# First layer's modulation in eight blocks of 256 shift and 256 scale columns, the first group of projections walking one block behind

## What is computed

```python
def mixer_layer(x, mod, norm_w, w_in, ...):
    shift, scale, gate = jnp.split(mod, 3, axis=-1)
    xn = rmsnorm(x, norm_w) * (1.0 + scale[:, None, :]) + shift[:, None, :]
    proj = xn @ w_in
    ...
# per layer, for both groups of tokens:
mod = jax.nn.silu(c) @ w_mod[l] + b_mod[l]        # w_mod[l]: 2048 x 6144 (shift, scale, gate)
```

## Time and profile before

| | us |
|---|---|
| median of three runs (2228.12 to 2229.08) | 2228.21 |
| profiled execution, whole | 2229.19 |
| its span | 2227.4 |
| PE busy in the span | 2174.2 |
| DVE busy | 1381.7 |
| ACT busy | 679.4 |

### The profile page before, as it was taken

How to read it: one execution, slowest core, us unless ns; L and a number is a source line. 1 busy time by engine, 2 the same in 40 slices (tenths; PEclk the granted TensorE clock), 3 DMA queues, 4 the chain that set the end, 5 groups by cost and what they waited for, 6 DMA issues and landing times.

```text
span 2227.4 us, 34005 instructions
## 1 busy us (share of the span) xinstructions
PE 2174.2 (98%) x13257; PEld 1922.4 (86%) x13257; DVE 1381.7 (62%) x2701; ACT 679.4 (31%) x1196; POOL 186.0 (8%) x125
## 2 busy tenths in 40 slices
PE   5999999999999999999989999999999999999998
PEld 2578877888999999999988888887799999999998
DVE  5469777986565666666457454555446666666654
ACT  4332222321343333533134222232133333344312
POOL 0000000000000000423321000000000000042331
PEclk9999999999999999999989999999999999999999
DMA  9988587664432333664444645444343333366444
GB/s 353 381 299 299 184 262 229 204 212 138 122 104 79 94 101 111 198 195 134 119 135 141 192 139 177 146 127 129 88 128 91 101 100 101 97 197 196 133 123 146
DMA packets 353200, 362.49 MB, mean 163 GB/s; under 512 B 17062, under 2 KB 259580, under 8 KB 352444
## 3 DMA queue, kind: packets, MB, share of 16 engines
q1 hardware_dynamic: 323536, 317.65, 45.8%
q10 hardware_dynamic: 29548, 43.25, 5.4%
HBM read 301.97 MB, written 58.88 MB: 162 GB/s over the span
## 4 chain that ended last, share of the span: by engine, by line
PE 91%; DVE 3%; ACT 2%; DMA 1%; issue 1%; ACTq 0%; SPq 0%; DVEq 0%
PE psP L732 32%; PE psP L767 20%; PE psP L784 10%; PE psT L742 8%; PE psO L973 5%; PE psP L904 3%; PE psO L946 2%; PE psT L915 2%; PE psO L693 1%; PE psT L973 1%; PE psT L650 1%; PE psO L650 1%; PE psO L797 1%; PE psP L985 1%; PE psP L674 1%
## 5 line engine op out<-in xcount | busy, mean ns | idle before, releaser
L732 PE MATMUL psP<-x_high,high 128*128 128x512 f32 x1024 | 413.1, 403 | 5.6 <-DVE x_low L1689 5.0
L732 PE MATMUL psP<-x_high,low 128*128 128x512 f32 x1024 | 400.7, 391 | 0.0
L732 PE MATMUL psP<-x_low,high 128*128 128x512 f32 x1024 | 400.7, 391 | 0.0
L1634 DVE SCALAR_TENSOR_TENSOR macc<-mraw,cond,macc 128x384 f32<-128x384 f32 (+1 forms) x960 | 389.7, 480 | 0.0
L1175 ACT ACTIVATE high<-raw 128x1024 fp32r<-128x1024 f32 x128 | 135.4, 1058 | 520.8 <-PE psT L742 507.0
L732 PEld LDWEIGHTS psP<-x_high,high 128*128 128x128 f32 x1024 | 193.2, 189 | 65.3 <-issue 24.0
L767 PE MATMUL psP<-x_high,high 128*128 128x320 f32 x1024 | 243.3, 319 | 0.5 <-issue 0.5
L767 PE MATMUL psP<-x_high,low 128*128 128x320 f32 x1024 | 233.3, 309 | 0.0
L767 PE MATMUL psP<-x_low,high 128*128 128x320 f32 x1024 | 232.7, 308 | 0.0
L732 PEld LDWEIGHTS psP<-x_high,low 128*128 128x128 f32 x1024 | 193.1, 189 | 41.6
L732 PEld LDWEIGHTS psP<-x_low,high 128*128 128x128 f32 x1024 | 193.5, 189 | 39.0 <-issue 1.9
(11 more groups left out here) (312 smaller groups left out, 3508.1 us busy)
## 6 DMA issues: line engine op xcount, KB each, us to landing
raw<-in_w_in_dram SPq DMA_DIRECT2D x128, 512.0 KB, 4.7
wmod<-in_w_mod_dram SPq DMA_DIRECT2D x32, 1024.0 KB, 9.5
mraw<-in_w_mod_dram SPq DMA_DIRECT2D x64, 512.0 KB, 4.3
mraw<-in_w_mod_dram SPq DMA_DIRECT2D x32, 1024.0 KB, 7.0
raw<-in_w_in_dram SPq DMA_DIRECT2D x32, 1024.0 KB, 6.1
raw<-in_w_out_dram SPq DMA_DIRECT2D x64, 512.0 KB, 4.4
old<-x_scratch SPq DMA_DIRECT2D x64, 320.0 KB, 3.0
proj_scratch<-stage ACTq DMA_DIRECT2D x64, 256.0 KB, 3.2
```

The source lines that it names most:

```text
L732: mm = pe.matmul(latent_ps[m], w[:, kk, cols], x[:, k, 0:DEC], start=(k == 0 and w is whole and x is x_high), stop=(k == KT - 1 and w is r ...
L1634: m = dve.scalar_tensor_tensor(acc[:, v, 0:width], mraw[hf][:, k, 0:width], c, acc[:, v, 0:width], ALU.mult, ALU.add)
```

## The change

The columns are cut in another way: block t now has the 256 shift columns and the 256 scale columns of the two input tiles 2t and 2t + 1. Each quarter of a block is loaded by two DMAs of 512 KB, one for each part, whose rows are 256 columns long. Two input tiles can be made ready after each block, where four were after every second. On PE, block 1 moves into the loop, with three pieces behind it; blocks 2 to 6 have five pieces each between and behind their quarters; block 7 has one behind each quarter, one more before its turn, and seven behind that. The turn of block t - 1 comes behind the first quarter of block t. ACT's and DVE's loops run over eight blocks of two tiles.

```diff
--- before.py
+++ after.py
@@ -72,20 +72,15 @@
 MOD_T = 3 * KT
 MOD_N = 512
 MOD_CHUNKS = 2 * D // MOD_N
-BLOCKS = KT // (MOD_N // P)
-BLOCK_K = MOD_N // P
-BLOCK_C = BLOCK_K // CHUNK_K
-
-
-def mod_at(t):
-
-    return (KT if t % 2 == 0 else 0) + t // 2 * BLOCK_K
+MOD_K = MOD_N // P
+BLOCKS = MOD_CHUNKS
+BLOCK_K = KT // BLOCKS
+assert BLOCK_K == CHUNK_K and MOD_K == 2 * BLOCK_K
 
 
 PIECES = GROUP_T + 1
 
-PIECES_AFTER, PIECES_LAST = [0, 1, 1, 1, 1, 1, 1, 0], 4
-assert sum(PIECES_AFTER) + PIECES_LAST == BLOCK_C * PIECES and len(PIECES_AFTER) == 8
+PIECES_AFTER = [[0, 0, 0, 3]] + [[1, 1, 1, 2]] * (MOD_CHUNKS - 3) + [[1, 1, 1, 1]]
 SAVES = 8
 SAVE_K = KT // SAVES
 SAVE_AT = {CHUNKS + RING + 2 * i: i for i in range(SAVES)}
@@ -335,7 +330,7 @@
             return pair[at // 2][:, at % 2 * KT // 2:(at % 2 + 1) * KT // 2, :].rearrange("p a b -> p (a b)")\
                 .rearrange("p (k n) -> p k n", n=GROUP_N)
         rs_ps = [psT[:, 0:512], psO[:, 512 + 2 * P:512 + 3 * P]]
-        mod_ps, mod_back = [psT[:, 512:512 + MOD_N], psO[:, 0:MOD_N]], psO[:, 512:512 + 2 * BLOCK_K]
+        mod_ps, mod_back = [psT[:, 512:512 + MOD_N], psO[:, 0:MOD_N]], psO[:, 512:512 + 2 * MOD_K]
         block = ctx.enter_context(nc.Block())
 
         q_back = psP[1][:, 0:TOK]
@@ -381,8 +376,10 @@
 
                 for q in range(4):
                     sp.wait_ge(s[f"wmod_used{q}"], t + SEED)
-                    sp.dma_start(wmod[q][:], wm[:, q * KT // 4:(q + 1) * KT // 4, mod_at(t) * P:mod_at(t) * P + MOD_N])\
-                        .then_inc(s[f"wmod_in{q}"], 16)
+                    for part in range(2):
+                        at = part * D + t * BLOCK_K * P
+                        sp.dma_start(wmod[q][:, :, part * BLOCK_K * P:(part + 1) * BLOCK_K * P],
+                                     wm[:, q * KT // 4:(q + 1) * KT // 4, at:at + BLOCK_K * P]).then_inc(s[f"wmod_in{q}"], 16)
 
             def front_chunk(l, n):
 
@@ -645,7 +642,7 @@
 
                 if q == 0 and t >= 2:
                     pe.wait_ge(s["mod_row"], t - 1)
-                pe.wait_ge(s[f"wmod_in{q}"], t * 16 + 16)
+                pe.wait_ge(s[f"wmod_in{q}"], t * 32 + 32)
                 for k in range(KT // 4):
                     mm = pe.matmul(mod_ps[t % 2][32 * k:32 * k + 2, :], cond[:, q * KT // 4 + k, :], wmod[q][:, k, :],
                                    start=(q == 0), stop=(q == 3), skip_group_check=True)
@@ -655,7 +652,7 @@
 
                 pe.wait_ge(s["mod_row"], t + 1)
                 pe.wait_ge(s["mod_taken"], t + SEED)
-                for j in range(BLOCK_K):
+                for j in range(MOD_K):
                     mm = pe.matmul(mod_back[:, 2 * j:2 * j + 2], mod_rows[t % 2][:, j * P:(j + 1) * P], fold[:, 0:2],
                                    start=True, stop=True)
                 mm.then_inc(s["mod_turned"], 1)
@@ -678,12 +675,6 @@
             pe.wait_ge(s["x_squared"], 2 * TT)
             pe.matmul(rs_ps[0], ones[:], r_a[:, 0:DEC], start=True, stop=True)
             pe.matmul(rs_ps[1], ones[:], r_a[:, DEC:TOK], start=True, stop=True).then_inc(s["stat_summed"], 1)
-            for q in range(4):
-                mod_quarter(1, q)
-                if q == 0:
-                    pe.wait_ge(s["x_squared"], 2 * TT + 2)
-                    mod_turn(0)
-            mod_turn(1)
 
             def gate_ranks():
 
@@ -837,19 +828,19 @@
 
                     pe.wait_ge(s["x_taken"], KT)
                     piece = 0
-                    for t in range(2, MOD_CHUNKS):
+                    for t in range(1, MOD_CHUNKS):
                         for q in range(4):
                             mod_quarter(t, q)
-                            if t % 2 == 1 and q == 0:
+                            if q == 0:
+                                if t == 1:
+                                    pe.wait_ge(s["x_squared"], 2 * TT + 2)
                                 mod_turn(t - 1)
-                            for _ in range(PIECES_AFTER[t % 2 * 4 + q]):
+                            for _ in range(PIECES_AFTER[t - 1][q]):
                                 block_piece(piece)
                                 piece += 1
-                        if t % 2 == 1:
-                            mod_turn(t)
-                            for _ in range(PIECES_LAST):
-                                block_piece(piece)
-                                piece += 1
+                    block_piece(piece)
+                    piece += 1
+                    mod_turn(MOD_CHUNKS - 1)
                     while piece < CHUNKS * PIECES:
                         block_piece(piece)
                         piece += 1
@@ -1137,8 +1128,9 @@
             def mod_take(t):
 
                 act.wait_ge(s["mod_turned"], t + 1)
-                act.activation(mod_raw[:, 0, mod_at(t):mod_at(t) + BLOCK_K, :].rearrange("p a b -> p (a b)"), mod_back,
-                               ACT.Copy).then_inc(s["mod_taken"], 1)
+                act.activation(mod_raw[:, 0, 0:2 * KT, :].rearrange("p (h k) v -> p h k v", h=2)
+                               [:, :, t * BLOCK_K:(t + 1) * BLOCK_K, :],
+                               mod_back.rearrange("p (h k v) -> p h k v", h=2, v=2), ACT.Copy).then_inc(s["mod_taken"], 1)
 
             for l in range(DEPTH):
                 for at, src in (
@@ -1240,10 +1232,9 @@
 
                 if l == 0:
                     for j in range(BLOCKS):
-                        for t in (2 * j, 2 * j + 1):
-                            mod_row(t)
-                            cast_chunk(t)
-                            mod_take(t)
+                        mod_row(j)
+                        cast_chunk(j)
+                        mod_take(j)
                         act.wait_ge(s["mod_ready"], j + 1)
                         for k in range(j * BLOCK_K, (j + 1) * BLOCK_K):
                             slot = k % 2
@@ -1699,16 +1690,14 @@
                     scale_block(0)
                     chunk_low(0)
                     for j in range(BLOCKS):
-                        dve.wait_ge(s["mod_taken"], 2 * j + 2 + SEED)
+                        dve.wait_ge(s["mod_taken"], j + 1 + SEED)
                         mod_sum([slice(j * BLOCK_K, (j + 1) * BLOCK_K), slice(KT + j * BLOCK_K, KT + (j + 1) * BLOCK_K)],
                                 2 * j + 2, j * BLOCK_K, BLOCK_K)
                         for k in range(j * BLOCK_K, (j + 1) * BLOCK_K):
                             split_x(k % 2, k // 2)
-                            if k % BLOCK_K == 1:
-                                chunk_low(BLOCK_C * j + 1)
                         if j + 1 < BLOCKS:
                             scale_block(j + 1)
-                            chunk_low(BLOCK_C * (j + 1))
+                            chunk_low(j + 1)
                 else:
                     for slot in range(2):
                         split_x(slot, 0)
```

## The result

| | before | after |
|---|---|---|
| median of nine runs each, us | 2228.21 | 2234.38 |
| lowest to highest, us | 2226.99 to 2229.43 | 2233.39 to 2236.43 |
| profiled execution, us (span) | 2229.19 (2227.4) | 2233.39 (2231.6) |

The changed kernel is slower: ratio 1.0029, 95% interval 1.0020 to 1.0037, or +6.2 us. The two profiled executions are 4.2 us apart.

The account below looks back on a forecast made before the run. PE was taken as the bound, busy 2174 of 2227.4 us. The last quarter's end 2.35 us later, less 1.0, plus 2.9 for one clock fall gave +4.25 us: 2232.5 us, range 2229.0 to 2236.8.

Parts of the forecast that it names:

- step 1: Start of the walk: PE's first projection piece begins at 47.0 us, not 51.7, after some 3 us of idle time.
- step 2: Blocks of the walk: 12.45 us each, turns no longer wait, last quarter of block 7 ends at 123.1 us, not 120.75.
- step 3: Modulation weight loads: 1 KB rows at 350 to 386 GB/s, 355 taken, so DMA adds nothing; +1.4 us kept for the range.
- step 4: After T, the last modulation quarter's end: late loads and ACT's copies hold back the second group; end moves by T's delay less 1.0 us.
- the rival that the late release hides: Second group's start is not held back: -3.2 us, 2225.0 us, or 2227.9 with a clock fall; chance 0.08.
- The rival of a fee per load: Modulation weight loads: each transfer pays up to 0.45 us, +12.2 us in all, 2240 us; chance 0.03.
- The clock: Idle stretches at 44 to 47 us and before the second group: one fall of the granted clock taken, +2.9 us.
- the rival without a fall: Clock falls at neither idle stretch: +1.35 us, or +2.75 with DMA at 350 GB/s, 2229.6 to 2231.0 us; chance 0.25.

Follow-up runs that it names:

- run 1: Changed kernel, but each quarter of modulation weights is one 1 MB load with 2 KB rows (other columns): 2232.46 us against 2228.53 before, ratio 1.0017.
- run 3: Kernel before, in its own order, but each quarter loaded as two halves with 1 KB rows: 2234.58 us against 2228.53, ratio 1.0026.
- run 5: Changed kernel, but SP issues the second projection group's first three chunks ahead of its wait for the last quarter: 2229.26 us against 2228.53 before, ratio 1.0006.
- run 6: Kernel before, with the second projection group's first three chunks issued ahead of the wait for the last quarter: 2228.59 us against 2227.91, ratio 1.0003.
- run 2: Changed kernel, but each quarter comes in two 512 KB loads with 2 KB rows (other columns): 2231.66 us against 2228.53 before, ratio 1.0017.
- run 7: Changed kernel with whole 1 MB, 2 KB-row loads and the second group's first three chunks issued early: 2227.20 us against 2227.91 before, ratio 0.9996.
- run 4: Changed kernel, but ACT takes the first group's latent tiles ahead of the second group's first two casts: 2231.07 us against 2227.91 before, ratio 1.0012.
- run 9: Kernel before with one piece ahead of the turns of blocks 3, 5, 7 and useless products in PE's early waits: 2227.20 us against 2227.94, ratio 0.9996.

## Why the prediction was right, and where it was off

Forecast 2232.5 us (2229.0 to 2236.8), measured 2234.38. The forecast called it no change by a hair (+0.19% against a bound of 0.2%), and gave slower by more 0.43; it is slower by more.

**The start** (step 1) was right: 46.72 against 47.0. The idle time ahead of it was 0.49, 1.96 and 0.47 us, 2.9 us in all, but not the one unbroken stretch that the argument on the clock was built on. **The pace** (step 2) was right, seen best where DMA doesn't bind: in run 1 the first piece is at 47.06 and T at 123.5, as against 47.0 and 123.1; and no turn waits.

**The transfers** (step 3) is the term that was mis-sized. I took 355 GB/s, which left T at 123.1; T was 126.3. Two parts. The rate: 352 GB/s with three loads of long rows among them; taking those out at 386 leaves some 348 for rows of 1 KB ((14.09 - 1.57) MB in 40 - 4.1 us), under the slower row that I had. I had taken a value between the two near rows, not the one row made of such packets alone, which said 350 and +1.4 us. And the start: I gave the early transfers half a microsecond; the last quarter of block 1 came at 45.21, not at 43.04, so 2.2 us. With both, 47.8 + 1.7 + 6.8 + 24.1/0.348 = 125.6 for the landing, against 125.3 measured. With long rows the new order delays T by 2.7 us (run 1), and short rows add 2.9 to that; in the old order short rows alone delay it by 5.6 (run 3), so the two are not costs that add up, and the later of PE and DMA sets T.

The traces show 386 GB/s for long rows and 348 for short ones, so a byte takes 11% longer. The estimate from the fixed cycles a packet that the Trainium skill states (DMA: Bandwidth & Descriptors, Why small descriptors are slow) was 4.5% longer; the traces don't agree, and the measurement decides.

**What hangs on T** (step 4) was right in each link: first cast at T + 13.8 (T + 14.3 forecast), tile 0 free at T + 18.0 (18.5), tile 2 at T + 21.85 (22.5), the wait for the last tiles 1.82 us (2.0), those at the second group 2.64 and 0.75 (3.3 and 1.2), end of the chunk at T + 26.1 (26.6). Runs 5 and 6 show that the link is the cause, and the rival that the late release hides fell with them. The rival of a fee per load fell with run 2.

**The clock** was off for the profiled pair: I booked one fall at 2.9 us; there was none in the profile of after. The forecast total (+4.25) and the profiled pair (+4.2) agree because the missing fall and the under-sized transfers nearly cancel: 5.6 us of delay of T, less 1.4, against 2.35 + 2.9 - 1.0. That agreement is luck. The profiled execution is the rival without a fall, which was priced at +1.35 to +2.75 us; the transfers' term is what that price lacked. In other runs of the same order falls were seen at either place: near 47 us in the profiles of runs 2, 5 and 7, at the second group in those of runs 1 and 2, behind the 1.8 us wait for the last tiles in that of run 4, nowhere in that of after. Each of those near 47 us cost 1.7 us of work, by the granted clock of the two stretches from 40 to 60 us (0.83 and 1.00 in run 5, 0.87 and 0.96 in run 2, 0.88 and 0.95 in run 7), not the 2.9 that I had booked. Among the nine runs of after the one with the highest mean clock (0.996) is the fastest, 2233.39, and it is the profiled one; but the five at 0.994 average 2234.7 and the three at 0.995 2234.6. It is thus possible, but not shown, that the clock makes up part of the 2 us between the profiled pair's difference and the medians'.

**The layers' boundary** shows how large such steps are. It is a place where the clock falls in both kernels at times that are not tied to the kernel's own. PE's last sums there take 1.28 us before, in time order:

```profile
1145.98 1.28 PE L821 MATMUL psO<-ones,r_b 128*128 128x1 f32 x10 [0.86 <-ACT r_b L1481]
```

They take 2.13 us after, at half clock:

```profile
1150.09 2.13 PE L812 MATMUL psO<-ones,r_b 128*128 128x1 f32 x10 [0.86 <-ACT r_b L1472]
```

That lengthens after, by 0.85 us, and is made up for further on (2079.1 us from the landmark to the end in both), so it doesn't explain the 2 us either. Half of the 2 us is that the profiled execution of before lies 1.0 us over its median, and half that the one of after lies 1.0 us under its own. What sets these apart stays open.

## What to carry to other kernels

Before cutting a load differently, price the new row length at a full queue: here 2 KB rows moved 386 GB/s and 1 KB rows 348, while the size of the load (512 KB or 1 MB) made no difference. When work is moved ahead of the last use of a buffer, look for what is issued only behind that use, and follow it to the next engine in order; in run 1's profile a walk that was shorter by 2.9 us was given back whole at that point, and issuing the independent loads ahead of the wait repaired it. Idle time or a low clock of an engine in a stretch that another resource bounds gave nothing here when it was removed (run 9).

## What was not expected of the hardware

Up to the loads of the last block the programs of after, run 4 and run 5 are the same, and PE stood idle for some 3 us ahead of the first piece in each; the granted clock fell there in the profile of run 5 (0.83 from 40 to 50 us) and in neither of the others. With the waits filled it did not fall in the one profile taken. Most of the loss read from the clock at the start was worth nothing in time (run 9). And 2 us of the kernel before whose packets were mostly of 1 KB, with some longer ones, gave 371 GB/s, where 1 KB packets alone gave 350 and the changed kernel some 348 for them over 40 us; a short stretch that mixes in longer rows is a poor price for a long one.
